# Ninth token tile of five projections in fourths of the columns, and the forget logits in fourths of the tokens, at four places of the TensorE array

## What is computed

```python
h = x @ w_in                       # zq zf zi zg (HGRN2 heads) | fq fk fv ff (FoX heads)
logf = log_sigmoid(ff + fbias)     # 8 forget logits per token
x = LN1(alpha*x + concat(hgrn2(zq,zf,zi,zg), fox(fq,fk,fv,logf)) @ w_out)
x = LN2(alpha*x + memory_attend(x, mem @ xa_wk, mem @ xa_wv) @ xa_wo)
x = LN3(alpha*x + hier_moe(x))     # top group, then top 2 of its 8 experts; 32 experts in all
```

## Time and profile before

| | before |
|---|---|
| median of three runs | 1997.67 us |
| profiled execution | 1996.47 us, span of the core 1994.1 us |
| TensorE busy, granted clock over the span | 1792.5 us (90%), 0.949 |
| VectorE busy | 750.0 us (38%) |
| ScalarE busy | 309.1 us (16%) |
| L427 (`rows`), all matmuls | x720, 318.4 us busy |
| L418 (`columns`), the eight-column ones among them | x48, 14.4 us busy |
| chain that ended last | y_blocks DMA 21%, TensorE 17%, VectorE 3% |

### The profile page before, as it was taken

How to read it: one execution, slowest core, us unless ns; L and a number is a source line. 1 busy time by engine, 2 the same in 40 slices (tenths; PEclk the granted TensorE clock), 3 DMA queues, 4 the chain that set the end, 5 groups by cost and what they waited for, 6 DMA issues and landing times. The chain is left out here.

```text
span 1994.1 us, 33667 instructions
## 1 busy us (share of the span) xinstructions
PE 1792.5 (90%) x14867; PEld 1131.6 (57%) x14867; DVE 750.0 (38%) x1089; ACT 309.1 (16%) x701; POOL 210.5 (11%) x196
## 2 busy tenths in 40 slices
PE   8999999999999779999998999939999999999650
PEld 4455568766654554445665665426666666666420
DVE  1111456534461653320012443364433333333227
ACT  1111223411010440111001111000101111111005
POOL 2100000000010420000000000032111111111016
PEclk9999999999999689999999999859999999999875
DMA  5341002001100203045111000349999999999826
GB/s 197 96 165 43 1 5 83 1 1 43 42 0 4 92 6 116 33 136 169 34 42 42 22 22 28 144 171 366 422 424 424 424 425 423 424 424 424 360 61 216
DMA packets 72862, 326.94 MB, mean 164 GB/s; under 512 B 13368, under 2 KB 27968, under 8 KB 59728
## 3 DMA queue, kind: packets, MB, share of 16 engines
q1 hardware_dynamic: 47840, 280.70, 35.1%
q10 hardware_dynamic: 17360, 22.03, 3.4%
q0 software_dynamic: 7584, 23.08, 3.2%
HBM read 288.05 MB, written 37.65 MB: 163 GB/s over the span
## 5 line engine op out<-in xcount | busy, mean ns | idle before, releaser
L785 PE MATMUL psum<-arena 128*32 128x256 f32 x6528 | 360.4, 380 | 32.0 <-issue 30.8
L418 PE MATMUL psum<-arena 128*128 128x352 f32 x1152 | 342.1, 460 | 0.0
L785 PEld LDWEIGHTS psum<-arena 128*32 128x32 f32 x6528 | 244.7, 110 | 146.5 <-issue 45.4
L427 PE MATMUL psum<-arena 128*128 128x512 f32 (+1 forms) x720 | 318.4, 601 | 5.9 <-DMA arena<-in_w_in 4.7
L418 PEld LDWEIGHTS psum<-arena 128*128 128x128 f32 x1152 | 219.3, 191 | 122.2 <-issue 1.1
L1348 DVE COPY arena<-psum 128x512 f32<-128x512 f32 (+7 forms) x135 | 90.9, 681 | 417.8 <-PE psum L427 221.6
L427 PEld LDWEIGHTS psum<-arena 128*128 128x128 f32 (+1 forms) x720 | 131.7, 185 | 177.4 <-issue 175.5
L794 PE MATMUL psum<-arena 128*32 128x256 f32 x3264 | 189.7, 389 | 24.1 <-DVE arena L1753 24.1
L794 PEld LDWEIGHTS psum<-arena 128*32 128x32 f32 x3264 | 125.4, 113 | 82.0 <-DVE arena L1753 25.5
L1743 DVE TENSOR_SCALAR arena<-arena 128x384 f32<-128x384 f32 x34 | 12.2, 360 | 357.1 <-ACT arena L1284 315.3
L1065 ACT ACTIVATE arena<-psum 128x128 f32<-128x128 f32 (+5 forms) x181 | 86.5, 495 | 349.8 <-PE psum L411 276.2
(11 more groups left out here) (243 smaller groups left out, 1402.1 us busy)
## 6 DMA issues: line engine op xcount, KB each, us to landing
arena<-in_moe_w_down SPq DMA_DIRECT2D x34, 2048.0 KB, 22.6
arena<-in_moe_w_gate SPq DMA_DIRECT2D x34, 2048.0 KB, 16.9
arena<-in_moe_w_up SPq DMA_DIRECT2D x34, 2048.0 KB, 22.0
arena<-in_w_in SPq DMA_DIRECT2D x7, 2048.0 KB, 9.8
y_blocks<-arena ACTq DMA_DIRECT2D x136, 96.0 KB, 2.0
y_blocks<-arena ACTq DMA_DIRECT2D x1, 8448.0 KB, 44.0
arena<-in_x_prompt SPq DMA_DIRECT2D x9, 512.0 KB, 3.3
arena<-in_w_out SPq DMA_DIRECT2D x2, 2048.0 KB, 11.0
```

What stands on the lines that cost most here:

```text
L418: last = mm(ps[0:m, c * BANK:c * BANK + THIRD], lhs(k), rhs[:, k, c * THIRD:(c + 1) * THIRD], start=(k == 0), stop=(k == KD - 1))
L427: last = mm(ps[0:n, c * 512:(c + 1) * 512], lhs(k), rhs(k, c), start=(k == 0), stop=(k == KD - 1))
L785: last = mm(out, xeT[:, b, a, k, :], gu[b][:, :, k, j * P:(j + 1) * P], start=(k == 0), stop=(k == KD - 1))
```

## The change

In `rows`, `values_quarter` and `out_half`, where the tile is the ninth, each matmul of 512 (or each pair of 512) columns becomes four matmuls of a fourth of the width: 128 columns for FK, FV and ZI, 256 for YO and YX. The jth puts its result into the PSUM rows 32j to 32j+32. The weights loaded, the 32 tokens, are the same for all four. The forget logits are computed by four matmuls of 264 tokens at the same four places, in one bank instead of three. VectorE's copy out becomes four instructions, each from 32 (or 8) rows of PSUM to the rows 0 to 32 (or 0 to 8) of one fourth of the destination. The `rhs` argument of `rows` is now the block of all columns, which `rows` cuts.

```diff
             def rows(key, banks, consumer, lhs, rhs, n, width=512):
                 ps = free_banks(pe, key, banks, consumer)
+                q = width // 4
                 for k in range(KD):
+                    if n == DEC:
+                        for j in range(4):
+                            last = mm(ps[DEC * j:DEC * j + DEC, 0:q], lhs(k), rhs(k)[:, q * j:q * j + q],
+                                      start=(k == 0), stop=(k == KD - 1))
+                        continue
...
-            columns(("FF",), [5, 6, 7], "dve", lambda k: w_ff[:, k, :], xT, m=FH)
+            ps = free_banks(pe, ("FF",), [5], "dve")
+            for k in range(KD):
+                for j in range(4):
+                    last = mm(ps[32 * j:32 * j + FH, 0:TQ], w_ff[:, k, :], xT[:, k, j * TQ:(j + 1) * TQ],
+                              start=(k == 0), stop=(k == KD - 1))
+            last.then_inc(pe_done, 1)
...
                 for k in range(2 * quarter, 2 * quarter + 2):
+                    if n == DEC:
+                        for j in range(4):
+                            last = mm(psum[DEC * j:DEC * j + DEC, bank * BANK:bank * BANK + P], xT[:, k, cols_of(t)],
+                                      w_fv[:, k, j * P:(j + 1) * P], start=(k == 0), stop=(k == KD - 1))
+                        continue
...
                 for k in range(4, 8) if fox else range(4):
+                    if n == DEC:
+                        for j in range(4):
+                            last = mm(psum[DEC * j:DEC * j + DEC, banks[0] * BANK:banks[0] * BANK + 256], mixT[:, k, cols_of(t)],
+                                      wrows[:, k, j * 256:(j + 1) * 256], start=(k == 4), stop=(k == 3))
+                        continue
...
+            def copy_rows(key, out, n):
+                ps = filled(dve, key)
+                if n == DEC:
+                    for j in range(4):
+                        last = V.tensor_copy(out[:, j * P:(j + 1) * P], ps[DEC * j:DEC * j + DEC, 0:P])
+                    take(last, key)
+                else:
+                    copy_job(key, out, ps[0:n, :])
...
-            take(TS(thirds(ffz[0:FH, :]), banked(ps[0:FH, :]), fbias[0:FH, :], None, ALU.add), ("FF",))
+            for j in range(4):
+                last = TS(ffz[0:FH, j * TQ:(j + 1) * TQ], ps[32 * j:32 * j + FH, 0:TQ], fbias[0:FH, :], None, ALU.add)
+            take(last, ("FF",))
...
-                take(STT(y, res, ALPHA, ps[0:n, :], ALU.mult, ALU.add), key)
+                if n == DEC:
+                    for j in range(4):
+                        c = slice(j * 256, (j + 1) * 256)
+                        last = STT(y[:, c], res[:, c], ALPHA, ps[DEC * j:DEC * j + DEC, 0:256], ALU.mult, ALU.add)
+                    take(last, key)
+                else:
+                    take(STT(y, res, ALPHA, ps[0:n, :], ALU.mult, ALU.add), key)
```

More of the change, by code:

```diff
@@ L38 @@
 THIRD = T // 3
+TQ = T // 4
 C_HG, C_FX = HH * HD, FH * FD
@@ L411, in turn, with columns @@
                 return nc.tensor.transpose(out, a, ident[0:n, 0:n])
-            def columns(key, banks, consumer, lhs, rhs, m=P):
+            def columns(key, banks, consumer, lhs, rhs):
                 ps = free_banks(pe, key, banks, consumer)
@@ L417, in columns @@
                     for c in range(3):
-                        last = mm(ps[0:m, c * BANK:c * BANK + THIRD], lhs(k), rhs[:, k, c * THIRD:(c + 1) * THIRD],
+                        last = mm(ps[:, c * BANK:c * BANK + THIRD], lhs(k), rhs[:, k, c * THIRD:(c + 1) * THIRD],
                                   start=(k == 0), stop=(k == KD - 1))
@@ L424, in rows @@
                 ps = free_banks(pe, key, banks, consumer)
+                q = width // 4
                 for k in range(KD):
+                    if n == DEC:
[3 more added lines that the diff above has]
+                        continue
                     for c in range(width // 512):
-                        last = mm(ps[0:n, c * 512:(c + 1) * 512], lhs(k), rhs(k, c), start=(k == 0), stop=(k == KD - 1))
+                        last = mm(ps[0:n, c * 512:(c + 1) * 512], lhs(k), rhs(k)[:, c * 512:(c + 1) * 512],
+                                  start=(k == 0), stop=(k == KD - 1))
                 last.then_inc(pe_done, 1)
@@ L453, in _ @@
                 w = weights(pe, "fk")
-                rows(("FK", t), [2 + t % 2], "dve", lambda k: xT[:, k, cols_of(t)], lambda k, c: w[:, k, :], n)
+                rows(("FK", t), [2 + t % 2], "dve", lambda k: xT[:, k, cols_of(t)], lambda k: w[:, k, :], n)
             pe.wait_ge(par_loaded, 16 * 9)
-            columns(("FF",), [5, 6, 7], "dve", lambda k: w_ff[:, k, :], xT, m=FH)
+            ps = free_banks(pe, ("FF",), [5], "dve")
+            for k in range(KD):
+                for j in range(4):
+                    last = mm(ps[32 * j:32 * j + FH, 0:TQ], w_ff[:, k, :], xT[:, k, j * TQ:(j + 1) * TQ],
+                              start=(k == 0), stop=(k == KD - 1))
+            last.then_inc(pe_done, 1)
             emptied(pe, ("FK", NT - 1))
@@ L473, in _ @@
             w_fv = weights(pe, "fv")
-            rows(("FV", 0), [6], "dve", lambda k: xT[:, k, cols_of(0)], lambda k, c: w_fv[:, k, :], P)
+            rows(("FV", 0), [6], "dve", lambda k: xT[:, k, cols_of(0)], lambda k: w_fv[:, k, :], P)
             pe.wait_ge(logf_ready, 1)
@@ L568, in _ @@
             for t in range(NT):
-                rows(("ZI", t), [6 + t % 2], "dve", lambda k: xT[:, k, cols_of(t)], lambda k, c: w[:, k, :], rows_of(t))
+                rows(("ZI", t), [6 + t % 2], "dve", lambda k: xT[:, k, cols_of(t)], lambda k: w[:, k, :], rows_of(t))
             def hg_state(h, c):
@@ L673, in _ @@
                         rows((key, t, c), [4 + t], "dve" if c == 0 else "act", lambda k: memT[:, k, t * P:(t + 1) * P],
-                             lambda k, _: w[:, k, :], P)
+                             lambda k: w[:, k, :], P)
                 if key == "MK":
@@ L729, in _ @@
                         weights(pe, "xo0")
-                    rows(("YX", u), [6, 7], "dve", lambda k: xoT[:, u % 2, k, 0:n],
-                         lambda k, c: wrows[:, k, c * 512:(c + 1) * 512], n, D)
+                    rows(("YX", u), [6, 7], "dve", lambda k: xoT[:, u % 2, k, 0:n], lambda k: wrows[:, k, :], n, D)
                 if 1 <= s <= NT:
@@ L1353, in _ @@
                 copy_job(("XT", t, 0), xT[:, 0:4, cols_of(t)], ps[:, :, 0:n])
-                copy_job(("FK", t), fk[0:n, t, :], filled(dve, ("FK", t))[0:n, :])
+                copy_rows(("FK", t), fk[0:n, t, :], n)
             dve.wait_ge(par_loaded, 16 * 9)
@@ L1405, in _ @@
                         n = rows_of(t)
-                        copy_job(("FV", t), fv[0:n, t, :], filled(dve, ("FV", t))[0:n, :])
+                        copy_rows(("FV", t), fv[0:n, t, :], n)
                     u = s - lag
@@ L1492, in _ @@
                 n = rows_of(t)
-                copy_job(("ZI", t), hv[0:n, t, :], filled(dve, ("ZI", t))[0:n, :])
+                copy_rows(("ZI", t), hv[0:n, t, :], n)
                 if t in (1, 2, 3):
```

## The result

The changed kernel's first four runs took 1961.76, 1964.03, 1985.77 and 1986.04 us, median 1974.9, against 1998.29 us for the kernel before (1995.52 to 2000.36); ratio 0.9878, 95% interval 0.9848 to 0.9909. I had forecast 1953.5, in a range from 1946 to 1966. So the sign was right and the size wrong: half of the runs are some 35 us faster, the other half 12. The mean granted clock tells the groups apart: 0.945 in the lower one, 0.933 or 0.934 in the upper. The kernel before shows one group only.

A forecast was written before the change was run, and what follows sets the result against it. TensorE bounds the kernel up to routing, weight loads the expert stage, which moves along. The terms sum to 44.1 us off the profiled 1996.47, 1952.4; as a median 1953.5, range 1946 to 1966.

The forecast's parts named there:

- rival A: Narrow matmuls: a group of 128 columns costs what one of 256 does; 4.8 us back, 1958.5; chance 0.10.
- rival B: Half clock beside existing waits (forget logits, YO's end, YX's end): 6 to 9 us back, 1959 to 1963; chance 0.10.
- Parts 1 and 2: FK's ninth tile and the forget logits, with the chain behind them: net 15.4 us less.
- Part 3: FV's ninth tile, in four attention steps: 4.8 us less, lower bound 3.5.
- Part 4: ZI's ninth tile, ahead of HGRN2, which moves along: 4.7 us less.
- Part 5: YO's first half, with tile 7's second half right behind: 5.1 us less.
- Part 6: YO's second half: gain cut to 2.2 us by a new wait of about 3 us on VectorE.
- Part 7: YX's ninth tile, before the router logits, at full clock: 11.9 us less, lower bound 8.5.
- rival D: Same 32 tokens as weights at all four places: matmuls don't overlap; some 40 us slower, 2038; chance 0.02.
- my own case: All parts gain as summed, places overlapping: own range 1949 to 1958 us; chance 0.70.

The follow-up runs named there:

- before with two: Kernel before plus two unused dense matmuls of 512 columns in front of attention: five runs at 2018.4 to 2026.6 us, ratio 1.0113.
- before with two and the spread: Kernel before plus two unused dense matmuls before attention, FV quarters at every other step from 19: eight runs 2000.6 to 2002.9 us, three 2009.6 to 2012.2.

## Why the prediction was wrong

**What it said of the mechanism was right.** Four places overlap for 128 columns too (rival A is out), TensorE's order passes each gain on, and the expert stage moves with its start and keeps its length (654.8, 656.0).

**The step that failed is the price of the clock.** My own sum had nothing for it. I had it as rival B, with a chance of 0.10 and "two or three more intervals at 2 us", next to the places that the change makes short, and held against it that the experts at four places keep their clock. I priced it by the earlier trace rows, a fall that one dense stretch ends at once. In attention no dense stretch follows at once: the light steps go on at half speed until dense quarters come, 41 us, 19.5 us of time. And I looked for it only where the change is, not at the stretches that the change moves. The page of before couldn't show how close that stretch was, as its clock there is 1.00 (9 in the earlier trace rows); the experiments showed it with 1.7 us of added work. I had also read the narrow spread of the three runs as a bound for what the clock may do, while it only showed that this kernel starts the stretch at a harmless moment. By their clock seven of the changed kernel's ten runs have this fall, and with two of the first four it moves the median out of my range; the three without it, 1961.8 to 1964.0, lie inside.

**The lower group, term by term**, 34.4 us of span instead of 44.1:

- Parts 1 and 2: 15.0, forecast 15.4. The matmuls were as computed (1.8 and 3.7 us), the wait behind the logits grew from 5.84 to 6.55. The four VectorE instructions take 1.99 us together, not the 1.6 that I had as the upper bound from a copy of the same size:

```profile
90.96 1.99 DVE L1399 TENSOR_SCALAR arena<-psum,consts 8x264 f32<-8x264 f32 x4 [1.19 <-PE psum L468]
```

- Part 3: 4.5, forecast 4.8. A step is 1.28 us, where it was 2.54, and the four copies at the end show as a wait of 0.38.
- Part 4: 5.1 up to HGRN2, forecast 4.7; but to YO 1.9 are lost again. Of them 0.8 lie inside HGRN2 and 1.1 at its end, where the clock stood at half. This too is a matter of the moment: in the second profile of the same kernel HGRN2 takes 98.2 us, 0.5 less than before. The window over its end in the first:

```profile
720.00:727.00 7.00, 6.42 (x13) 3.42 (x14) 0.88 (x1) 2.75 (x3) 0.00 (x0) 0.76 0.00 0
```

- Part 5: 4.5 to the transposes of tile 6, forecast 5.1; YO's first 0.6 us of loss belong to the same half clock.
- Part 6: 2.2, to the tenth what was forecast, with the new wait of 2.85 us on VectorE, forecast about 3. But then 2.2 are lost at the next step, because this wait is followed by half clock (16 transposes in 3.65 us instead of 2.03):

```profile
842.39 1.93 PE L661 MATMUL psum<-arena 128*32 128x256 f32 x32
847.18 1.71 PE L412 MATMUL psum<-consts,arena 128*128 128x128 f32 x8 [2.85 <-DVE arena L1599]
850.10 3.65 PE L412 MATMUL psum<-consts,arena 128*128 128x128 f32 x16 [1.21 <-ACT arena L1087]
```

and the window over it:

```profile
850.00:857.00 7.00, 5.79 (x21) 4.33 (x22) 2.78 (x4) 2.54 (x4) 0.97 (x6) 0.68 1.04 398
```

- Part 7: the ninth tile's YX takes 5.3 us, between the 3.5 and 6.9 that I gave, since the clock fell in it; I had written "It follows tile 7's work, so I take the full clock", which the trace of before already spoke against (0.90 in the earlier trace rows). Its four VectorE instructions take 1.70 us, 0.5 more and not 0.2. The stage gives 11.2 instead of 11.9, but 1.5 of these come from ahead of the ninth tile's YX, where nothing was changed and less stood at half clock; from YX on it is 9.8.

```profile
1246.69 5.35 PE L430 MATMUL psum<-arena 128*32 128x256 f32 x64
1251.97 1.17 PE L412 MATMUL psum<-consts,arena 128*128 128x128 f32 x8
1252.11 1.70 DVE L1581 SCALAR_TENSOR_TENSOR arena<-arena,psum 32x256 f32<-32x256 f32 x4 [5.11 <-PE psum L430]
```

- Routing and experts: 0.9 and 1.2 lost; L792, which is L770 of before, takes 1.31 us instead of 0.76, at clock 0.50. That row also shows that my reading of it in the earlier trace rows was one at the full clock.
- 2.3 us are the later start.

One slip in rival D: it sets a narrow matmul at 34 ns in the sum, where 0.12 us a group of four makes 30. Measured are 28 (64 in 1.77 us), so the comparison with 107 stands.

So two places that became short next to a wait, YO's end and YX, lost about 2 us each to the clock, in both profiles of the changed kernel (YX 5.35 and 4.86 us, the 16 transposes at YO's end 3.65 in either), as rival B said of them. The 2.5 us at the end of HGRN2 and YO's start come in one of the two only. B and my own case both came true in the lower group, and the range covered only B's price for near places.

**What stays open**: why the stretch keeps the clock at one position of the rhythm and loses it at another is shown only by its effect. The ten runs of the changed kernel divide 3 to 7, and its two profiles lie at two positions (1.7 and 2.9 us); with one profile of each kind, the share itself isn't explained. Some runs lose another 8 us (FK, FV and ZI alone; before with two, once; before with two and the spread); only one of these was profiled, and why it happens in some runs isn't known. Nor did I measure each of the five projections by itself.

## What to carry to other kernels

Narrow work on a part of the array gains nearly its full factor when it is put at four places, down to 128 columns, and on the critical path the gain arrives. But look beforehand at every stretch where TensorE does only short or narrow matmuls: any change ahead of it, faster or slower, moves the moment at which it begins, and here a stretch without dense work then ran at half the clock until dense work returned. Mix dense matmuls that have slack into such stretches (here this took the 41 us away and cost about 2 us in attention), and time several executions with their mean clock beside them, since one profile may show either group.

## What the runs showed of the hardware

- TensorE's granted clock can be 0.50 for 41 us while the profile has the engine busy for 10.00 of every 10 us and no wait (37 instead of 66 matmuls in 10 us).
- The same instructions keep 1.00 or fall to 0.50 according to when they begin: with 0, 1.7 and 3.4 us more of dense work ahead, 0 of 59, 5 of 5 and 0 of 11 runs had the slower form.
- Within one trace all changes of the granted clock stand on one regular beat. From the light stretch's beginning to the next beat it was 0.9 to 1.7 us in six executions that kept the clock, 2.9 to 3.4 us in three that lost it.
- Four VectorE instructions of 8x264 from PSUM take 1.99 us where one of 8x1056 took 1.30; four of 32x256 take 1.70 where one of 32x1024 took 1.21; four copies of 32x128 take 1.18 where one of 32x512 took 0.68. Three more instructions cost 0.5 to 0.7 us.
- Groups of four matmuls of 128 columns, with four weight loads of 32 columns, take 0.11 us (16 groups in 1.77 us from start to start), no more than by their columns.
